# The last tile's unscaled rows go to the router, and the prompt's list is spread amid the last output products

## The reference, cut to what matters

```
x  = x + gate1 * (merged @ w_out)
h2 = rms_norm(x, norm2_g) * (1 + scale2) + shift2
aff = softmax(h2 @ w_router, axis=experts)         # (L, 16)
gate, idx = top_k(aff.T, 2 * L // 16)              # each expert picks 64 sample and 16 prompt tokens
xs = h2[idx];  hid = silu(xs @ w_gate) * (xs @ w_up);  out = (hid @ w_down) * gate
x  = x + gate2 * scatter_add(out, idx);  y = rms_norm(x, final_norm_g)
```

## Time and profile before

| | |
|---|---|
| three runs | 1976.9 us median, 1974.73 to 1981.16 |
| the profiled execution | 1968.58 us, span 1966.8 us |
| PE, DVE, ACT, POOL busy | 1896.0, 1199.5, 394.4, 407.8 us |
| mean granted PE clock | 0.988 |
| DMA | 647.59 MB, mean 329 GB/s over the span |

### The profile page before, as it was taken

One profiled execution on the slowest core, in us unless ns is written; L12 is line 12 of the kernel. 1 busy time (PEld: TensorE's weight loads), 2 busy tenths in 40 slices (PEclk: granted clock), 3 DMA queues, 4 the chain that ended last, 5 costly groups with the idle time before them and its releaser, 6 DMA issues.

```text
span 1966.8 us, 64418 instructions
## 1 busy us (share of the span) xinstructions
PE 1896.0 (96%) x28661; PEld 1423.3 (72%) x28661; DVE 1199.5 (61%) x1976; ACT 394.4 (20%) x909; POOL 407.8 (21%) x406
## 2 busy tenths in 40 slices
PE   8999999999998999999999999999999999999996
PEld 5888899999884788788878566655556565556663
DVE  3532441231556767777677776767777676777674
ACT  4332332222331112111121111111111121111113
POOL 3032009100412130220311213031120302113021
PEclk8999999999999999999999999999999999999998
DMA  8244532212389999999999999999999999999997
GB/s 338 85 158 159 177 114 80 90 50 86 122 346 351 413 406 419 407 411 415 407 417 411 412 414 407 419 407 411 416 412 414 407 419 408 411 415 412 415 410 300
DMA packets 150464, 647.59 MB, mean 329 GB/s; under 512 B 11420, under 2 KB 56344, under 8 KB 134024
## 3 DMA queue, kind: packets, MB, share of 16 engines
q1 hardware_dynamic: 134576, 617.71, 78.3%
q0 software_dynamic: 15648, 29.02, 5.1%
q10 hardware_dynamic: 184, 0.06, 0.0%
HBM read 632.47 MB, written 14.40 MB: 329 GB/s over the span
## 4 chain that ended last, share of the span: by engine, by line
PE 56%; DMA 28%; DVE 9%; issue 3%; SPq 2%; ACT 1%; POOL 1%; POOLq 0%; DVEq 0%; ACTq 0%
DMA ring<-in_w_exp_gate_dram 25%; PE bank L2064 16%; PE bank L2493 12%; PE bank L2521 7%; PE bank L2510 6%; DVE sums L1790 4%; PE bank L2503 4%; PE bank L2185 3%; PE bank L2332 3%; SPq L584 2%; DVE hid_t L1855 2%; DMA ring<-in_w_exp_down_dram 1%; PE bank L2418 1%; PE bank L2035 1%; PE bank L2046 1%
## 5 line engine op out<-in xcount | busy, mean ns | idle before, releaser
L1790 DVE TENSOR_TENSOR sums<-ring 128x704 f32<-128x704 f32 x744 | 609.4, 885 | 249.7 <-DMA ring<-in_w_exp_gate_dram 209.2
L2493 PE MATMUL bank<-ring,hid_t 128*32 128x256 f32 x8184 | 473.5, 384 | 34.1 <-DVE hid_t L1862 33.4
L2521 PE MATMUL bank<-ring,xs_t 128*32 128x352 f32 x5952 | 448.0, 459 | 0.2 <-issue 0.2
L2493 PEld LDWEIGHTS bank<-ring,hid_t 128*32 128x32 f32 x8184 | 282.2, 111 | 198.5 <-DVE hid_t L1862 40.4
L2521 PEld LDWEIGHTS bank<-ring,xs_t 128*32 128x32 f32 x5952 | 248.7, 110 | 184.8 <-issue 123.3
L2510 PE MATMUL bank<-sums,xu_a 128*32 128x176 f32 x5952 | 252.9, 313 | 0.2 <-issue 0.2
L2510 PEld LDWEIGHTS bank<-sums,xu_a 128*32 128x32 f32 x5952 | 208.6, 110 | 18.6 <-issue 0.6
L847 POOL TENSOR_TENSOR small<-kpow 128x2 f32<-128x2 f32 x31 | 13.3, 428 | 968.4 <-DVE out_rows L1923 806.2
L1224 ACT ACTIVATE v_both<-bank 128x176 f32<-128x176 f32 x31 | 9.8, 317 | 843.5 <-PE bank L2510 843.5
L2064 PE MATMUL bank<-act_hi,wt_hi 128*128 128x320 f32 x448 | 138.8, 310 | 0.8 <-DVE rtmp L1582 0.8
L1332 DVE TENSOR_TENSOR wt_lo<-raw_t,wt_hi 128x2048 fp32r<-128x2048 f32 x25 | 57.5, 2301 | 134.4 <-ACT wt_hi L944 134.4
(11 more groups left out here) (389 smaller groups left out, 2351.6 us busy)
## 6 DMA issues: line engine op xcount, KB each, us to landing
ring<-in_w_exp_gate_dram SPq DMA_DIRECT2D x127, 1408.0 KB, 25.2
ring<-in_w_exp_up_dram SPq DMA_DIRECT2D x127, 1408.0 KB, 27.7
ring<-in_w_exp_down_dram SPq DMA_DIRECT2D x96, 1536.0 KB, 25.8
ring<-in_w_exp_down_dram SPq DMA_DIRECT2D x32, 1024.0 KB, 30.1
raw_t<-in_w_ada_dram SPq DMA_DIRECT2D x16, 1024.0 KB, 5.3
raw_t<-in_w_in_dram SPq DMA_DIRECT2D x14, 1024.0 KB, 5.1
a_raw<-in_w_ada_dram SPq DMA_DIRECT2D x8, 1024.0 KB, 16.8
raw_t<-in_w_branch_gate_dram SPq DMA_DIRECT2D x8, 1024.0 KB, 5.4
```

Of the source, the lines that this page charges most:

```text
L1790: nc.vector.tensor_tensor(sums[:, (N_SUM * i + j) % SUM_SLOTS], w[:, k, :, n, :], w[:, kk, :, nn, :], ALU.add if sign > 0 else ALU.subtrac ...
L2493: ins = mm(bank[5 + x // 2][c * Q:(c + 1) * Q, x % 2 * DC:(x % 2 + 1) * DC], hid_t[:, f, x * Q:(x + 1) * Q], w[:, j, c * DC:(c + 1) * DC], ...
L2521: ins = mm(bank[UP_BANK[x]][c * Q:(c + 1) * Q, 0:FC], xs_t[:, x, k * Q:(k + 1) * Q], w[:, kk, c * FC:(c + 1) * FC], start=k == 0, stop=k = ...
```

## The change

Only the last tile (i = 4), two lists and one small product are touched.

1. PE makes shift2 @ w_router for the sample once, 8 products between the first and second block of the output product (`shift_product`), and DVE copies the 16 values per row to `sw`.
2. For the last tile DVE no longer waits for the root before the router's input: right behind each half of the residual it makes u = x * gs2 (`last_scaled`). PE transposes u, ACT copies, and the router's product runs on u. DVE then takes the reciprocal of the root, copies the three other tiles' logits out of their bank, and makes the last tile's logits as r * product + sw (`last_logits`). The softmax reads all four from SBUF.
3. h2 of the last tile is finished by two instructions behind the softmax (`last_shifted`), in place.
4. The prompt's indices are spread and listed inside `last_chunk(1, 0)` and ahead of `residual(4)`; the prompt's gates are spread behind the last router and copied behind the last tile's h2. POOL's gather of the prompt's rows waits for the indices alone, as before.
5. ACT copies the first half of the last transposed tile ahead of the root and the second half behind it; the router starts on a half. The 15 products of `keep_warm` around the last transposes are gone. The signal that frees two ring slots (`e_used`) moves from the fourth router to the first transpose of the last tile.

```
     for lt in ORDER:
+        if lt == ORDER[4]:
+            out += [(("ix", 1, 0), "dve")]
         out += [(("h2", lt, 0), "act"), (("h2", lt, 1), "act")]
...
-        if lt == ORDER[3]:
-            out += [(("ix", 1, 0), "dve"), (("ga", 1, 0), "dve")]
+    out += [(("ga", 1, 0), "dve")]
...
             norm_root(3)
             h2_to_t(3)
+            h2_to_t(4, (0,))
             norm_root(4)
-            h2_to_t(4)
+            h2_to_t(4, (1,))
...
+            def last_scaled(c):
...
+                dve.wait_ge(s_x2, 2 * i + c + 1)
+                nc.vector.tensor_tensor(h2[:, i % 2, cs], x2[:, X2_POS[lt], cs], gs2_b[0][:, cs], ALU.mult).then_inc(s_u, 1)
+
+            def last_logits():
...
+                dve.wait_ge(s_sqrt, NT + i + 1)
+                tick(nc.vector.reciprocal(small[:, 24 + lt:25 + lt], small[:, 16 + lt:17 + lt]))
+                dve.wait_ge(s_lg, NT - 1)
+                for n in (ORDER[1], ORDER[2], ORDER[3]):
+                    nc.vector.tensor_copy(aff[:, n, :], bank[LG_BANK[n]][:, n * NE:(n + 1) * NE])
+                dve.wait_ge(tr_read["dve"], TR_DVE["sw", 0, 0])
+                dve.wait_ge(s_lg, NT)
+                tick(nc.vector.scalar_tensor_tensor(out=aff[:, lt, :], in0=bank[LG_BANK[lt]][:, lt * NE:(lt + 1) * NE],
+                                                    scalar=small[:, 24 + lt:25 + lt], in1=sw[:], op0=ALU.mult, op1=ALU.add))
...
+            prompt_lists()
             residual(4)
-            prompt_lists()
-            second_norm(4)
-            softmax(1, 0, NS)
+            last_logits()
+            softmax(1, 0, NS, aff[:, 0:NS, :])
+            last_shifted()
+            prompt_gates()
             dve.wait_ge(e_gath, 16)
             dve.wait_ge(s_h2, 2 * NT)
...
             last_chunk(1, 0)
             last_chunk(1, 1)
+            h2_transpose(4, (0,))
             router(3)
-            pe.wait_ge(s_topp, 1)
-            prompt_spread(("ix", 1, 0), top_f)
+            h2_transpose(4, (1,))
+            pe.wait_ge(wo_read, 2 * NT)
+            router(4)
             prompt_spread(("ga", 1, 0), top_v)
-            keep_warm(11, 7)
-            h2_transpose(4)
-            keep_warm(4, 7)
-            router(4)
             aff_transpose(0, range(NS))
```

More of the change, by code:

```diff
@@ L245 @@
 WO_BANKS = ((7, OLDEST[0]), (OLDEST[1], OLDEST[2]), (OLDEST[3], OLDEST[4]))
-LG_BANK = {lt: OLDEST[4] if lt == NS else OLDEST[3] for lt in range(NT)}
+LG_BANK = {lt: OLDEST[4] if lt == NS else OLDEST[1] if lt == ORDER[-1] else OLDEST[3] for lt in range(NT)}
 TR = Plan(tr_units(), (5, 6))
@@ L1667, in second_norm, with softmax @@
                     nc.vector.tensor_tensor(h2[:, i % 2, cs], h2[:, i % 2, cs], sh2_b[cnd][:, cs], ALU.add).then_inc(s_h2, 1)
[L1669 to L1672 removed]
+            def softmax(group, lo, n, lg):
                 rows = aff[:, lo:lo + n, :]
@@ L1704, in _ @@
             second_norm(2)
-            softmax(0, NS, 1)
+            dve.wait_ge(s_lg, 1)
+            softmax(0, NS, 1, bank[LG_BANK[NS]][:, NS * NE:NT * NE].rearrange("p (a b) -> p a b", a=1))
             residual(3)
```

59 lines of the change are left out of this document (46 added, 13 removed).

## The result

| | before | change |
|---|---|---|
| median of 12 runs each, taken in turn | 1975.52 us | 1980.03 us |
| ratio of the two, 95% interval | | 1.0016 [1.0009, 1.0023] |
| profiled execution, span | 1968.58, 1966.8 us | 1978.66, 1976.8 us |

One of the change's twelve executions was a slow one (2028.92 us, granted clock 0.941 against 0.990 to 0.993); the ratio leaves it out, and without it the median is 1979.85.

A forecast was written before the change was run, and what follows sets the result against it. The weight stream's start, hanging on the first gather, was taken as the bound. Gather -1.2 us plus 0.3 for SP's fifth piece gave -0.9: 1967.7 us profiled, median forecast 1976.0, range 1972.5 to 1980.0.

The forecast's parts named there:

- The stream sets the end: From 616 us on: the end is when the weight stream flows for good plus fixed bytes at 412 GB/s.
- the stream hangs on the first gather: Transition before the loop: later weight pieces wait for the first gathered rows; gather forecast about 608.6, 1.2 us earlier.
- The list path: Router, softmax, top_k and lists: `idx_all` done at 606.5 instead of 609.51, bringing 3.0 us by itself.
- Upstream: PE work ahead of the last x: added shift product 0.3 us, spread of indices 0.3; last x at about 586.1.
- The store path: Last h2 store, then gate2 loads on POOL: h2 ready 2.55 us later, landing 603.1, POOL free at 608.3.
- near the lower bound: Landing of h2's store: lower bound 602.6 if only the weights' backlog counts, upper bound 604.9; 603.1 taken.
- rival 1: Last h2 store takes as long as before from a later start; gather 0.6 us later, 1977.5 us; chance 20%.
- rival 3: First expert products: PE's clock falls, each 4 us costing 2; decides only over 12 us low; +6 us or more, 1983; 5%.
- the likeliest case: The main forecast for the transition: gather 1.2 us earlier, -0.9 us in total, median 1976.0 us; chance 45%.
- The 15 products without a use were no work: `keep_warm` around the last transposes: removing its products was claimed to cost nothing.
- rival 2: Stores take equal turns with the weights: landing 598.1 to 599, list decides, gather 606.8, -3.0 us, 1973.9; chance 13%.
- The sum: Whole kernel: gather -1.2 us plus 0.3 for running into SP's fifth piece gives -0.9 us.

The follow-up runs named there:

- e2_h2_early: The change with the last tile's h2 finished in DVE's wait for the last router, not behind the softmax; ratio to the kernel before 1.0001.
- e4_held: The kernel before with POOL's last x and h2 stores held until the softmax is done; ratio to the kernel before 1.0016.
- e6_h2_g2: The change with h2 finished in the wait for the last router and the gate2 loads issued ahead of the last stores; ratio to the kernel before 1.0002.
- e11_change_copy: The change run once more, unedited, as a second measurement; ratio to the kernel before 1.0018.
- e10_gather_first: The change with h2, last x store and gate2 loads earlier, SP's fifth piece held until the first gathered rows landed; ratio to the kernel before 0.9986.
- e9_small: The change with h2, last x store and gate2 loads earlier, plus two wide unused products behind the prompt rows; ratio to the kernel before 0.9991.
- e1_copy: The kernel before, copied with no edit, as a control; ratio to the kernel before 1.0003.
- e8_all: The change with h2, last x store and gate2 loads earlier, plus seven wide unused products behind the prompt rows; ratio to the kernel before 1.0008.
- e7_before_g2: The kernel before with only the eight gate2 loads moved ahead of the last stores; ratio to the kernel before 1.0005.
- e12_before_gf: The kernel before with x and gate2 loads early and SP's fifth piece held until the first gathered rows landed; ratio to the kernel before 1.0020.
- e3_fill: The change with 22 short unused products behind the last prompt rows; ratio to the kernel before 1.155, 2277.77 us.

## Why the prediction was wrong

The forecast failed on two terms of its sum: the landing of h2's store, put at 603.1 and measured at 604.4, and PE's clock, put at nothing and measured at 1.9 us. The late landing helped to bring the low clock (e2_h2_early is without both, e4_held has both).

- **The stream sets the end: borne out, with a rival that was not tested by itself.** The loop's rate is unchanged, and the megabytes by 700 us give the differences of profiled executions on one chip within some 0.3 us, apart from e6_h2_g2. The rival, which the prediction doesn't name, is that PE's own work sets the end, for which the chains speak, with PE at 91 to 95% in most traces. By it the end would move with the start of the first expert products and the extra time of the first 96. From e11_change_copy to e10_gather_first these are 5.4 + 2.6 = 8.0 us; the profiled time moved by 6.1, the megabytes said 6.3. So the stream has the better fit, on two pairs of traces (the other is e9_small with 8.3, 6.6 and 6.8). But "the stream hangs on the first gather" was too narrow: it hangs on the landing of the gathered rows, and that on the piece in front of them (e6_h2_g2, e10_gather_first), and on PE's clock behind them.
- **The list path: right.** Top_k was forecast at 593.8 and came at 592.91; `idx_all` at 606.5 and came at 605.48. That it came earlier is the luck of one execution, whose last x was complete at 584.72, not 586.1. Counted from the last x the list was forecast after 20.4 us and came after 20.8 and 20.4 in the two traces of the change (24.0 in both of before).
- **Upstream: right.** From the first output product of the last stage (L2332, L2377) to the last x it is 67.6 and 67.7 us in the two traces of before and 68.1 in both of the change: 0.4 more, forecast 0.6.
- **The store path: here the number failed.** I issued the store at 593.5 and landed it at 603.1, "near the lower bound", since the weights would be through at 601.7 and the last 0.3 MB would need 1.4 us alone. The weights were nearly through at 602, as forecast. But the stores did not run beside them from 592.95 on at 17.1%: they stood still for 3.8 us, then took turns packet for packet, and at 602 had 0.05 MB left, not 0.3. What held the landing until 604.4 was the tail: 22 packets in the 2 us from 602 on, at 59 GB/s in all, and 0.4 us more until the landing, 11.6 us behind the issue. That is rival 1, to which I gave 20%: the store takes as long as before from a later start. Over all kernels stores issued between 589 and 592 take 11.4 to 13.7 us and those of 592.4 and later, in the kernels without other moves, 9.7 to 11.6: a store that leaves 1 us later lands some 0.6 us later. I had given 2.55 us of delay a landing only 0.8 later; the measured ones (592.82 against 590.54 of e1_copy, landings 604.4 and 603.1) say 1.3 for 2.3, from a landing that was itself 0.7 later than in the first trace. With the 5.2 us of POOL behind it, the gather went at 609.91 and not 608.6.
- **The clock (rival 3): right in size, wrong in my conclusion.** "Each 4 us of it cost 2 us" is what happened: 96 products at 9.19 in place of 7.31 us. But I charged it with nothing in the likeliest case, and named as its condition a low stretch of over 12 us. Four microseconds were enough to add 1.9 us. What I had not asked is where PE rests once the list is early: its prompt products follow the list, so they ended at 607.85 and not 613.29, while the rows did not come sooner. The earlier list and the late rows together made the 5.82 us of rest; with the rows 1.8 us earlier, e2_h2_early had 2.45, also because its clock was low from 604 to 608 (0.57) and the prompt products ended only at 609.46. "The 15 products without a use were no work" was not the fault: e2_h2_early does without them at full clock.
- **Equal turns (rival 2): right in the turns, wrong in the time.** The two queues moved 228 and 228 packets from 595 to 600 in before and 269 and 266 from 596 to 602 in the change, with 58% of the bytes in the weights' packets. It had the landing at 599 at the latest, and the earliest of all was 601.6, for what it leaves out: 3.8 us until the first packet, and the tail. The rule of the Trainium skill, "DMA: Bandwidth & Descriptors", section "Queues, rings and completion order", is that an engine takes turns between queues by packet; the trace agrees with it, and where the prediction said that it did not, the window of the earlier trace rows was too wide.
- **The sum.** Upstream 0.4, the gather counted from the last x 0.9, the clock 1.9, together 3.2; measured 3.2 (interval 1.8 to 4.5). In the second traces it is 0.4, 0.0 and 2.6, together 3.0; measured 3.6. Two traces each make this a sum that fits, no more.

## What to carry to other kernels

Where one wait has two feeders 2 us apart, shortening the later one is worth at most those 2 us, and what is moved in front of the earlier one (here the finishing of h2, 1.9 us late, for which a store waits) eats them up; put it into the idle time ahead of the shortened path, as e2_h2_early does. A small transfer that others wait for should not be issued behind a large one that nobody waits for yet: with 1.4 MB of weights held back some 5 us the gather flew 2.80 us and not 6.55, in the fastest kernel of all, though the times don't separate this step from the other moves. And when a path gets shorter, look at what else it drags forward: work that used to fill PE's wait may now end early and leave the clock to fall.

## What the runs showed of the hardware

- **Two queues took turns packet for packet**, whatever the packets' size: 228 and 228 (0.87 and 1.21 MB) in before, 211 and 212 (0.23 and 1.17 MB) in e8_all, where small packets of one queue held up the 4 KB packets behind them.
- **POOL's stores under full load** had no packet for 3.7 to 4.2 us after the first was issued (eleven of the traces; in e6_h2_g2, e7_before_g2 and e12_before_gf other transfers of POOL stood in between), and a thin tail at the end: in the change 0.05 MB of 1.05 after 602, with the DMA engines at share 0.15, and the landing at 604.4. What makes the delay and the tail, the runs don't show.
- **A gather of 0.13 MB** (128 partitions of 256 columns) took 2.80 us alone, 2.89 to 3.99 when the 1.4 MB piece had gone 4.2 to 6.0 us before it (e7_before_g2, e4_held, e2_h2_early, the change, e1_copy), 4.5 at 2.4 us behind it (e8_all), and 5.3 and 6.55 at 1.8 us (e9_small, e6_h2_g2).
- **The granted clock** was 1.00 for the first expert products after rests of 0.35, 0.86, 0.93, 1.59 and 2.45 us (e10_gather_first, e7_before_g2, e3_fill, e1_copy, e2_h2_early), and at its lower level for part of them after 2.07, 2.25, 2.65, 4.12, 5.29 and 5.82 us (e12_before_gf, e4_held, e9_small, e6_h2_g2, e11_change_copy, the change). Of the four between 2.07 and 2.65 us three came out low and one full.
- **Instruction fetches**: 313 packets in place of 42 and 15.5% more time for 22 more PE products ahead of a loop, 15 more than in the kernel before (e3_fill). Where between 0 and 15 more it begins was not tried. The Trainium skill, "Runtime: NRT & Kernel Launch", section "Instruction fetch mechanics", says that instructions stream in blocks and that a taken branch to a target outside the window forces a fetch; the trace agrees, and here the price was some 10 us for each of 31 steps (307 us more than the kernel before on the same chip) where the section calls crossing a block mostly hidden.
